# One slot later for VectorE's convolution taps in the state space stage

## The reference, cut to what matters

```
xBC = silu(causal_depthwise_conv_3(xBC, conv_w, conv_b))     # 4 taps: sum(xp[:, k:k+L] * w[k]) + bias
xs, Bm, Cm = xBC[:1024], xBC[1024:1536], xBC[1536:2048]      # 16 heads of 64; 4 groups, state 128
y  = ssd_chunked(xs, dt, A, Bm, Cm) + D * xs                 # 8 chunks of 128 positions per group
y  = gated_group_rmsnorm(y, z)                               # y*silu(z), mean square over 256 channels
```

## Time and profile before

| | us |
|---|---|
| median of 3 runs | 3053.16 (3051.78 to 3054.39) |
| the profiled execution | 3053.03 |
| its span | 3051.2 |
| mean granted TensorE clock | 0.991 of full |

### The profile page before, as it was taken

One profiled execution on the slowest core, in us unless ns is written; L12 is line 12 of the kernel. 1 busy time (PEld: TensorE's weight loads), 2 busy tenths in 40 slices (PEclk: granted clock), 3 DMA queues, 4 the chain that ended last, 5 costly groups with the idle time before them and its releaser, 6 DMA issues.

```text
span 3051.2 us, 37933 instructions
## 1 busy us (share of the span) xinstructions
PE 2957.6 (97%) x15222; PEld 2393.2 (78%) x15222; DVE 1650.4 (54%) x2710; ACT 1165.2 (38%) x1987; POOL 994.7 (33%) x716
## 2 busy tenths in 40 slices
PE   8999999999999999999999999999999999999998
PEld 7876668887878888887888866777877888888887
DVE  6989760025546654233233577777656645534436
ACT  3125662222441121223333267546546533332344
POOL 3210002223417785234531212321111234442542
PEclk9999999999999999999999999999999999999999
DMA  4110001113413333113342201332222155443323
GB/s 135 49 40 22 15 15 52 50 51 120 134 60 88 88 96 97 43 51 124 104 133 66 60 29 56 125 113 69 61 66 70 50 150 126 150 141 110 107 80 111
DMA packets 257408, 252.19 MB, mean 83 GB/s; under 512 B 16304, under 2 KB 198704, under 8 KB 256208
## 3 DMA queue, kind: packets, MB, share of 16 engines
q1 hardware_dynamic: 232624, 198.15, 21.7%
q10 hardware_dynamic: 24608, 51.62, 5.2%
HBM read 209.22 MB, written 38.80 MB: 81 GB/s over the span
## 4 chain that ended last, share of the span: by engine, by line
PE 80%; DVE 10%; ACT 5%; DMA 2%; issue 2%; POOL 1%; SPq 1%; ACTq 0%; DVEq 0%
PE psum L579 24%; PE psum L581 23%; PE psum L580 23%; PE psum L585 3%; DMA arena<-in_w_in 2%; DVE arena L2989 2%; DVE arena L2446 1%; PE psum L792 1%; ACT WS L1260 1%; PE psum L969 1%; PE psum L762 1%; PE psum L993 1%; DVE XL L2311 1%; DVE arena L2401 1%; SPq L3731 1%
## 5 line engine op out<-in xcount | busy, mean ns | idle before, releaser
L3293 POOL TENSOR_TENSOR WS<-arena,WS 128x1024 fp32r<-128x1024 f32 (+1 forms) x295 | 722.8, 2456 | 1649.7 <-ACT WS L1260 1649.6
L579 PE MATMUL psum<-XH,WS 128*128 128x512 f32 x2600 | 1031.1, 397 | 16.7 <-ACT arena L2070 3.5
L581 PE MATMUL psum<-XH,WS 128*128 128x512 f32 x2600 | 1015.8, 391 | 0.0
L580 PE MATMUL psum<-XL,WS 128*128 128x512 f32 x2600 | 1014.6, 390 | 0.0
L579 PEld LDWEIGHTS psum<-XH,WS 128*128 128x128 f32 x2600 | 489.8, 188 | 134.4 <-issue 13.2
L1260 ACT ACTIVATE WS<-arena 128x1024 fp32r<-128x1024 f32 (+1 forms) x295 | 308.2, 1052 | 745.0 <-PE psum L581 258.4
L581 PEld LDWEIGHTS psum<-XH,WS 128*128 128x128 f32 x2600 | 489.2, 188 | 103.8
L580 PEld LDWEIGHTS psum<-XL,WS 128*128 128x128 f32 x2600 | 490.2, 189 | 96.8
L579 PE MATMUL psum<-WS,XH 128*128 128x512 f32 x960 | 377.7, 393 | 12.1 <-POOL WS L3293 8.7
L580 PE MATMUL psum<-WS,XH 128*128 128x512 f32 x960 | 374.6, 390 | 0.0
L581 PE MATMUL psum<-WS,XL 128*128 128x512 f32 x960 | 374.6, 390 | 0.0
(11 more groups left out here) (305 smaller groups left out, 2907.1 us busy)
## 6 DMA issues: line engine op xcount, KB each, us to landing
arena<-in_w_in SPq DMA_DIRECT2D x85, 512.0 KB, 3.8
arena<-in_w_out SPq DMA_DIRECT2D x48, 512.0 KB, 3.7
arena<-in_w_in_even SPq DMA_DIRECT2D x48, 512.0 KB, 4.0
arena<-in_w_out_even SPq DMA_DIRECT2D x32, 512.0 KB, 3.7
h_spill<-arena ACTq DMA_DIRECT2D x24, 512.0 KB, 3.1
arena<-s_table SPq DMA_DIRECT2D x8, 1536.0 KB, 6.8
arena<-in_w_in_odd SPq DMA_DIRECT2D x18, 512.0 KB, 3.8
s_table<-arena SPq DMA_DIRECT2D x32, 256.0 KB, 3.0
```

Source lines behind the costliest of these rows:

```text
L579: e.matmul(ps, wh, xh, start=start, stop=False)
L580: e.matmul(ps, wh, xl, start=False, stop=False)
L581: return e.matmul(ps, wl, xh, start=False, stop=stop)
L3293: e.tensor_tensor(lo, x, hi.bitcast(F32), SUB).then_inc(*w.up("w_lo", u))
```

## The change

In DVE's program, a slot no longer makes the taps of its own piece. It keeps them in `late` and makes the taps of the piece before. The taps of the last piece are made at the start of the slot that follows the eight. The other four engines' programs, the buffers, the waits named in the code and every instruction stay.

```
             def prep(g):
+                late = None
                 for i in range(4):
-                    yield from proj_cm(1, lambda _, half: taps(g, i, half, RAW3[half]))
+                    for half, _ in enumerate(proj_cm(1)):
+                        if late:
+                            taps(g, *late)
+                        late = (i, half, RAW3[half])
+                        yield
+                taps(g, *late)
```

## The result

The median is 3057.57 us (3052.92 to 3060.05, 20 runs) against 3051.88 before (3047.69 to 3056.18, 20 runs); the ratio is 1.0017, with an interval of 1.0011 to 1.0024. That is 5.2 us more by the ratio (the medians lie 5.7 us apart), clear of zero and inside the 0.2% that the prediction called no change; 3.0 us more were forecast. The spans of the two profiled executions are 6.5 us apart, of which 0.93 lie ahead of the stage, in code that is the same.

A forecast was written before the change was run, and what follows sets the result against it. PE, busy 97%, was taken as the bound, so only its waits and slowed clock had a price. 4.2 + 0.1 + 0.1 - 1.4 = +3.0 us on 3053.0 gave 3056.0 us; range 3046 to 3066.

The forecast's parts named there:

- What the order takes away: Stage: DVE's 33.5 us wait for L1999 goes, front no longer stands behind its slot's product; otherwise PE would bound.
- What it adds, the cycle: Silu waits for late taps, the next front for the exponential behind it: 18.3 us per two rounds, PE needs 15.3.
- Two signs: DVE waiting 3 to 4 us for L2013 after each silu; in group 0 every second PE L1058 waiting 2 to 3.
- Group 0: First group of the stage: the cycle puts its last L1075 at 2149.55 instead of 2145.34, +4.2 us.
- Groups 1 and 2: With gate steps between silus, the gain at 2191's stall is lost by the group's end: +0.1 us each.
- The clock term: Ends of groups 1 and 2: more low clock falls into PE's idle time, 0.7 us back each (0 to 1.7).
- The rule on the table load: Against the change: a 1.38 us drain per table switch behind a wait would cost group 0 8.3 us more.
- A: Rival, chance 0.20: the cycle holds in groups 1 and 2 too, 4.2 us each, no clock back; 3065.6 us.
- B: Rival, chance 0.11: group 0 as forecast, groups 1 and 2 keep what they win at 2191; -2.6, 3050.4 us.
- C: Rival, chance 0.08: the silu wait binds nowhere, PE bounds the stage, waits and missing clock go; -18.6, 3034.4 us.
- D: Rival, chance 0.08: nothing moves, DVE's waits in the stage only change their name; 3053 us.
- E: Rival, chance 0.03: longer table change, a 1.28 us gap behind each waited load, 7.7 us on top; 3063.7 us.

The follow-up runs named there:

- experiment 3: The changed kernel with ACT's silu also moved one place later, behind the raw copy of the next block's first piece; 0.9936, 3031.38 us.
- experiment 4: The kernel before with only ACT's silu moved behind the raw copy, DVE's taps where they were; 0.9933, 3031.82 us.
- experiment 5: The changed kernel with the silus of groups 1 to 3 replaced by plain copies that need no table; 0.9956, 3038.25 us.
- experiment 6: Extra 1.04 us ACT pass ahead of each of twelve silus: in the changed kernel 1.0055, 3069.57 us; in the kernel before 1.0027, 3062.34 us.
- experiment 2: The changed kernel with only first halves' taps late, a block's two sets made together in its second piece's slot; 0.9952, 3038.12 us.
- experiment 1: The changed kernel with taps late only for group 1's pieces, beside group 0's chunks; 1.0013, 3057.23 us against 3052.64 before.

## Why the prediction was right, and where it was off

*What the order takes away*: right. The wait for L1999 is gone, and with the silu out of the way the stage becomes PE's (experiments 3 and 4, where the granted clock of the stage reads 1.00 and PE's waits of the stage's rounds come to 3.7 and 2.6 us).

*What it adds, the cycle*: right in its place and its size, term by term (7.23, 2.00, 2.24, 2.45, 2.00 and 2.40 us in the timeline above). 18.3 us were forecast from silu to silu and 18.32 measured; the first silu's load was forecast for 2086.3 and stands at 2087.22 less the 0.93 of the start. Experiments 5 and 6 take from it and add to it about what they should (16.08 and 19.41), and experiment 2 removes it by leaving the silu's input on time. Two signs were off in size: DVE waits 4.85 us for the exponential and not 3 to 4, and PE's three waits in group 0 are 2.47, 2.59 and 1.13 us and not all 2 to 3.

*Group 0*: +4.2 forecast, +4.29 measured, and experiment 1 has it alone. *Groups 1 and 2*: +0.1 each forecast, +0.06 and 0.00 measured. What is won at the stall of 2191.74 is lost by the end, as laid out: the silus of group 1 were forecast for 2179.9, 2201.1 and 2220.7 and stand at 2179.6, 2201.0 and 2220.7, less the 5.22 us by which the group begins later. That this comes from the silus and not from the gate steps was not tried by itself.

*The clock term* was off, and with it nearly all of the difference between 3.0 and 5.2 us: -0.7 each was forecast, -0.50 and +1.36 measured. I took group 2's clock from group 1's window, though the two windows before read 0.59 and 0.79. The first, longer wait did put 1.2 us more of the low stretch into idle time behind group 1; behind group 2 the low stretch doubled. But like waits were followed by 6.8, 3.4 or no us at the low level (last section), so one execution of each kernel can neither confirm nor refute a term of 0.7. That the -0.50 came out near it is luck. The terms less the start give 4.29 + 0.06 - 0.50 + 1.36 + 0.35 = 5.6 us, against 5.2 by the ratio.

*The rule on the table load*: the trace agrees with the row, not with the longer price. With the load behind a wait of 4.88 us, the silu still starts 1.30 us after the load does (2105.53 to 2106.83), and 1.29 or 1.30 all twelve times. A drain of 1.38 us at each switch, as the Trainium skill states (ScalarE: Activation LUTs, section What ACT_TABLE_LOAD costs), would have made the cycle 21 us, an estimate from that page's figure (18.3 + 2 x 1.38); 18.32 was measured, and taking both switches out (experiment 5) gave back 2.24.

*Rivals*: A (the cycle binds in groups 1 and 2 too) and B (they keep their gain) are excluded by the +0.06 and 0.00; C by the twelve waits; D by the interval; E by the load. What the prediction did not see is that C's 18.6 us were to be had, by one edit on ACT and in either order of DVE. I put the old stalls down to DVE's order alone; experiment 2 takes half of them away by DVE's order (12.4 to 6.2 us) and experiment 4 most by ACT's (to 2.6), so they came of the two orders together, with POOL's pass on top.

## What to carry to other kernels

When work is moved one slot later, ask who waits for its *result*, on which queue that waiter stands, and what stands behind it there: the move took away a wait of 33.5 us in sum and made one of 58.2, on an engine that was busy for 38% of the span. Add up the cycle that the new wait closes and compare it with the bound engine's time for the same rounds; 18.3 against 15.3 told the result to 0.1 us a group. And put what nobody waits for soon (here a silu whose block is needed many rounds later) behind the copy that the next engine needs now: that alone gave 20.8 us. Then ask how much room is left: a further pass of 1 us on ACT ahead of each silu still cost 7 us of them.

## What the runs showed of the hardware

Three taps took 2.33 us alone and 3.15 with POOL's pass of 2.4 us beside their start. How much longer they take goes by how far they reach into that pass: when POOL's pass ends 0.55 us (experiment 4), 1.03 (the kernel before), 1.50 or 2.06 us (both experiment 3) after the taps begin, they take 2.67, 3.15, 3.62 or 4.18 us, and when it ends 0.2 us after or less, 2.33. No trace of this case shows another pair. So the taps are longer by the time that they lie beside the pass, less 0.2 us.

The low stretch of TensorE's clock behind like waits of PE (0.64 or 0.65, then 1.72 us) was 6.8 us behind group 1 and 3.4 behind group 2 in the kernel before, and none and 3.4 in experiment 1. Each such wait carries up to 3 us of chance (25.88 against 22.96 us for the same products).
